# Feature stages of a two-layer decoder trunk: matmuls issued as two wide and two narrow, in place of one wide and one narrow in turn

## The reference, cut to what matters

```python
for i in range(DEPTH):                       # 2 layers
    hn = rms_norm(h, pre_mix_g[i])
    y = conformer_conv(hn, ...) if i == 0 else diff_attention(hn, ...)
    h = h + rms_norm(y, post_mix_g[i])
    u = causal_dwconv(rms_norm(h, pre_ffn_g[i]) @ ffn_w_in[i], ffn_w_dw[i])   # "up" product
    g, up = jnp.split(u, 2, axis=-1)
    f = (jax.nn.silu(g) * up) @ ffn_w_out[i]                                  # "down" product
    h = h + rms_norm(f, post_ffn_g[i])
    gate = sigmoid(rms_norm(h, ple_pre_g[i]) @ ple_w_gate[i] + ple_b_gate[i])
    h = h + rms_norm(gate * (p[i] @ ple_w_proj[i]), ple_post_g[i])
# diff_attention: q, k, v = split(x @ w_qkv); softmax(q k') twice, weighted; ... @ w_o
```

## Time and profile before

| | |
|---|---|
| time, median of three | 2470.36 us |
| time of the profiled execution | 2471.12 us |
| its span, first to last instruction | 2469.2 us |
| mean granted TensorE clock | 0.989 of full speed |
| busy: PE / PEld / DVE / ACT / POOL | 97% / 83% / 66% / 50% / 1% |
| mean busy share of the 16 DMA engines over the queue of weights | 55.6% |

### The profile page before, as it was taken

How to read it: one execution, slowest core, us unless ns; L and a number is a source line. 1 busy time by engine, 2 the same in 40 slices (tenths; PEclk the granted TensorE clock), 3 DMA queues, 4 the chain that set the end, 5 groups by cost and what they waited for, 6 DMA issues and landing times.

```text
span 2469.2 us, 38655 instructions
## 1 busy us (share of the span) xinstructions
PE 2407.0 (97%) x12274; PEld 2059.0 (83%) x12274; DVE 1632.9 (66%) x2208; ACT 1240.9 (50%) x1777; POOL 33.1 (1%) x58
## 2 busy tenths in 40 slices
PE   8999899999999999999899999999999999999997
PEld 7888678888888878878788887888888888888876
DVE  5988667777777754456655676577777777544465
ACT  3333545555555544446544455465656556444463
POOL 1000000000000000000000000000000000000000
PEclk9999999999999999999999999999999999999999
DMA  7552455566655665556475544656556656655553
GB/s 262 167 166 69 145 162 173 185 196 192 190 180 186 198 205 193 195 168 216 143 218 185 178 154 145 196 155 188 185 187 195 193 183 185 215 194 194 192 192 137
DMA packets 364721, 448.16 MB, mean 182 GB/s; under 512 B 27108, under 2 KB 273030, under 8 KB 363488
## 3 DMA queue, kind: packets, MB, share of 16 engines
q1 hardware_dynamic: 362576, 436.36, 55.6%
q0 software_dynamic: 2064, 10.79, 1.3%
HBM read 444.95 MB, written 2.10 MB: 181 GB/s over the span
## 4 chain that ended last, share of the span: by engine, by line
PE 91%; issue 4%; DVE 2%; ACT 1%; DMA 1%; POOL 0%; SPq 0%; DVEq 0%; ACTq 0%; POOLq 0%
PE ps L1343 31%; PE ps L1345 16%; PE ps L1378 11%; PE ps L1380 11%; PE ps L1379 11%; PE ps L1422 9%; PE ps L1323 1%; DMA gain<-in_post_ffn_g 1%; PE ps L1517 0%; PE ps L1531 0%; DVE h L896 0%; DVE w_lo L854 0%; PE ps L1480 0%; ACT v_conv L656 0%; ACT w_hi L542 0%
## 5 line engine op out<-in xcount | busy, mean ns | idle before, releaser
L854 DVE TENSOR_TENSOR w_lo<-raw,w_hi 128x1024 fp32r<-128x1024 f32 x760 | 925.5, 1223 | 649.4 <-ACT w_hi L542 629.6
L542 ACT CAST w_hi<-raw 128x1024 fp32r<-128x1024 f32 x760 | 792.5, 1049 | 746.6 <-PE ps L1380 378.0
L1343 PE MATMUL ps<-x,w_hi 128*128 128x512 f32 x3328 | 1161.9, 395 | 3.1 <-issue 3.1
L1345 PE MATMUL ps<-x,w_lo 128*128 128x256 f32 x3328 | 929.6, 279 | 0.0
L1343 PEld LDWEIGHTS ps<-x,w_hi 128*128 128x128 f32 x3328 | 625.4, 188 | 147.2 <-issue 4.1
L1345 PEld LDWEIGHTS ps<-x,w_lo 128*128 128x128 f32 x3328 | 629.2, 189 | 0.0
L1378 PE MATMUL ps<-w_hi,mid 128*128 128x512 f32 x704 | 274.2, 390 | 3.1 <-DVE w_lo L854 3.1
L1379 PE MATMUL ps<-w_lo,mid 128*128 128x512 f32 x704 | 274.0, 389 | 0.0
L1380 PE MATMUL ps<-w_hi,mid 128*128 128x512 f32 x704 | 274.0, 389 | 0.0
L1378 PE MATMUL ps<-w_hi,x 128*128 128x512 f32 x640 | 254.9, 398 | 7.2 <-DVE x L1051 3.8
L1379 PE MATMUL ps<-w_lo,x 128*128 128x512 f32 x640 | 250.6, 392 | 0.0
(11 more groups left out here) (160 smaller groups left out, 1278.3 us busy)
## 6 DMA issues: line engine op xcount, KB each, us to landing
raw<-in_ffn_w_in SPq DMA_DIRECT2D x704, 256.0 KB, 3.1
raw<-in_ffn_w_out SPq DMA_DIRECT2D x352, 256.0 KB, 3.5
raw<-in_attn_w_qkv SPq DMA_DIRECT2D x192, 256.0 KB, 2.9
wg<-in_conv_w_pw SPq DMA_DIRECT2D x128, 256.0 KB, 4.0
raw<-in_ple_w_gate SPq DMA_DIRECT2D x128, 256.0 KB, 3.5
raw<-in_conv_w_pw SPq DMA_DIRECT2D x64, 256.0 KB, 3.5
raw<-in_attn_w_o SPq DMA_DIRECT2D x64, 256.0 KB, 3.4
raw<-in_ple_w_proj SPq DMA_DIRECT2D x16, 256.0 KB, 3.6
```

The lines of the kernel that those rows point to most:

```text
L542: nc.scalar.copy(w_hi[:, u % RING], raw[:, u % RING]).then_inc(hi_split, 1)
L854: nc.vector.tensor_tensor(w_lo[:, u % RING], raw[:, u % RING], w_hi[:, u % RING].bitcast(F32), ALU.subtract).then_inc(split_done, 1)
L1343: mm(ps[:, 4 * s + f], w_hi[:, u % RING, q, columns], x[:, kt].rearrange("p a t -> p (a t)"), start=kt == 0, stop=False)
L1345: ins = mm(ps[:, 4 * s + f, 0:T], w_lo[:, u % RING, q, columns], x[:, kt, 0], start=False, stop=kt == KT - 1)
```

## The change

Inside a unit the eight pairs (wide, narrow) are taken two at a time. For the two pairs `a` and `b` the order wide a, narrow a, wide b, narrow b becomes wide a, wide b, narrow a, narrow b. Two neighbouring pairs always have the same input block and differ in the output block, so they write different PSUM banks. Number, shape and operands of the matmuls are unchanged, and so is the last instruction of a unit, the one that counts it as used.

```diff
-                    for q in range(UNIT_KT):
-                        kt = UNIT_KT * j + q
-                        for f in blocks:
-                            columns = slice(P * f, P * (f + 1))
-                            mm(ps[:, 4 * s + f], w_hi[:, u % RING, q, columns], x[:, kt].rearrange("p a t -> p (a t)"),
-                               start=kt == 0, stop=False)
-                            ins = mm(ps[:, 4 * s + f, 0:T], w_lo[:, u % RING, q, columns], x[:, kt, 0],
-                                     start=False, stop=kt == KT - 1)
+                    def wide(q, f):
+                        kt, columns = UNIT_KT * j + q, slice(P * f, P * (f + 1))
+                        return mm(ps[:, 4 * s + f], w_hi[:, u % RING, q, columns], x[:, kt].rearrange("p a t -> p (a t)"),
+                                  start=kt == 0, stop=False)
+
+                    def narrow(q, f):
+                        kt, columns = UNIT_KT * j + q, slice(P * f, P * (f + 1))
+                        return mm(ps[:, 4 * s + f, 0:T], w_lo[:, u % RING, q, columns], x[:, kt, 0],
+                                  start=False, stop=kt == KT - 1)
+
+                    order = [(q, f) for q in range(UNIT_KT) for f in blocks]
+                    for at_n in range(0, len(order), 2):
+                        wide(*order[at_n])
+                        wide(*order[at_n + 1])
+                        narrow(*order[at_n])
+                        ins = narrow(*order[at_n + 1])
                     return ins
```

## The result

The changed kernel takes 2477.6 us in the median of 20 runs (2474.0 to 2482.1), the kernel before 2471.7 us in the median of its 20 (2467.3 to 2475.6). The ratio is 1.0026, with a 95% interval of 1.0019 to 1.0032: slower by about 5.9 us, and clear of noise. It lies inside the forecast range and just inside the band of 0.3% that I had called the same. The forecast of exactly no change was 2470.4 us: 7.2 us too low, of which 1.3 are the median of the kernel before, which moved from 2470.4 in three runs to 2471.7 in 20.

What follows compares the result with a forecast made beforehand. The prediction took TensorE's matmul pace as the bound; 453.4 + 119.6 + 119.6 ns made 692.6 per four as before, a change of 0 and 2470.4 us against the median. Its own range was 2463 to 2478, for 8 in 10 2459 to 2490.

Steps and rivals of the forecast that it cites:

- my three outcomes: Whole kernel: the same within 0.3%, chance 0.64; slower by more, 0.22; faster by more, 0.14.
- my own test: Windows of up 0, 400 to 800 us: 2310 matmuls again; wrong if the count moves by more than 7.
- sum of zero: Four matmuls in the feature stages: 453.4 + 119.6 + 119.6 = 692.6 ns, as before, so 0 us over 1664.
- The bound: Whole kernel: TensorE sets the end for 91% of the span, the two changed lines holding 31% and 16%.
- The narrow matmul before a narrow one: New step inside a unit: its weight load stays covered, so it takes 119.6 ns as before a wide one.
- rival C: Narrow-to-narrow step: a second short slot can't cover its load; 115.5 us slower, giving 2586; chance 0.05.
- The two wide matmuls: Wide-to-wide and wide-to-narrow steps in a unit: 226.7 ns each as in the token stage, 453.4 ns for both.
- Rival A: Up stages: qk's slow rhythm of 352.5 ns a pair spreads there; 17.5 us slower, giving 2488; chance 0.18.
- Rival D: qk: loses its slow rhythm; 3.2 us faster, giving 2467; no chance of its own, counted inside the forecast's 0.62.
- Rival B: Feature stages: the fixed price belongs to changes of kind; 44.3 us faster, giving 2426; chance 0.13, whole or in part.

Runs made afterwards that it cites:

- e7: Changed kernel with VectorE's wait for the gain in the down stages moved to just ahead of its first multiplication: 2471.0 us, ratio to before 1.0002.
- e6: Kernel before with VectorE's wait for the gain in the down stages moved to just ahead of its first multiplication: 2466.1 us, ratio 0.9980.
- e3: Changed kernel with all eight wide matmuls of each unit first, then all eight narrow ones: 2477.9 us, ratio to before 1.0021.
- e9a: Kernel before with one extra 128-column transpose into an idle bank behind the first chunk of each feature stage: 2480.5 us, one run.
- e4: Changed kernel with the new order kept in qk alone and the old order in both up stages: 2471.6 us, ratio to before 1.0006.
- e13: Changed kernel with one extra transpose behind the first chunk of each feature stage: 2477.6 us, one run.

## Why the prediction was right, and where it was not

The range held the time and the likeliest of my three outcomes came, but by little, and the pace failed my own test: I had said that a count off by more than 7 in the window of up 0 would prove me wrong, and it is off by 11. The prediction was right on what bounds the kernel and on the loads; its sum of zero was wrong. That the time stayed in the range owes much to luck: a loss of 4.8 us in the up stages, a gain of 2.2 in qk and some 3 us of clock that I had not thought of.

*The bound.* Right: TensorE still holds 91% of the chain, and a pace that makes 5 us makes 5 us of time (e7 against e6, 4.8).

*The narrow matmul before a narrow one, 119.6 ns.* Right in what mattered, that its load is covered; rival C (115.5 us) is out. The step itself is 114.6 ns in the changed kernel and 120.0 in the long runs of e3. The Trainium skill's page "TensorE: Matmul & The Clock Gate", section "LDWEIGHTS (loading the stationary operand)", gives a load its columns over 1.2 GHz, an estimate of 107 ns. Two loads begun 0.11 us apart here agree with it. By the Trainium skill's section "Back-to-back issue gap" of that page, columns over 2.4 GHz plus 2.5 ns each, a pair is an estimate of 325 ns. That fits no order of the fp32r matmuls: the quickest takes 346.7.

*The two wide matmuls, 453.4 ns, and the sum.* This is the step that failed. I took the steps of like kinds from stages where like had followed like for long and added them to those of the mixed stage, as if each step had its own price. In the changed kernel the two wide steps take 232.9 + 233.3 = 466.2 ns, 12.8 more than the 453.4 of the sum, and the two narrow ones 230.4, 8.8 less than its 239.2. By the counts the four are 2 x 348.0 = 696.0 ns, not 692.6: 3.4 ns x 1408 = 4.8 us over the up stages that the sum has at nothing. Even the old pair was split wrongly, as 226.7 and 119.6 where up 0 has 230.1 and 116.6. The 226.7 of the token stage returns only from the sixth wide matmul of a run on (e3).

*Rival A.* Its mechanism is real, shown by e9a and e6: the old order has two patterns at a fixed clock. But the new order did not fall into that one; it has a pattern of its own at about a quarter of the price (1.7 for 6.2 ns), the same in ten stages of four programs (the changed kernel, e4, e7, e13). Its limit was worked out too low: 7.4 us over the 1408 fours of the up stages are 5.3 ns for four, not 4.5. *Rival D* came in at two thirds: qk gained 2.2 of the 3.2 us, by losing the slow pattern. *Rival B* is out: like after like still pays the fixed price in a long run (120.0 for 106.7 ns in e3), and what the narrow steps of the changed kernel saved, the wide ones more than took back.

*What I did not count.* The clock. I treated it as the same on both sides; it makes up to 3.3 of the 5.9 us, on runs with a scatter of 4 us either way. Nor did I see that a gain in qk can be lost again at the head of up 1, as in e4.

*Open.* What makes the patterns. They depend on the order of kinds, not of banks, and on the moment after an interruption for the old order; the series 0 or 6.2, 1.7, 4.3, 2.4 is described by a cost behind each change of kind that levels off after some five wide matmuls, but why there is such a cost is not shown. Nor is why the clock at the head of up 1 goes with the pace of qk.

## What to carry to other kernels

When an engine is the bound and the change only reorders its instructions, don't add up prices of single steps from different stages; count instructions in a long window of each stage, and look whether equal code runs at unequal pace in two stages, for then the pace may be a pattern that small things can shift. A change of under 0.5% should be judged by such counts and by runs of equal mean clock, not by medians alone; and a gain in one stage should be looked for again in the next ones, where the clock may take it back. And look for pauses too: one wait moved to its first real user took away two, of 2.2 and 0.9 us, and the kernel gained 5.1 us, about as much as the order cost; part of that came, in the profile, by way of qk's pattern.

## What the runs showed of the hardware

- In a long run of its own kind, an fp32r matmul takes its columns at 2.4 GHz plus 13.3 ns: 226.7 for 512 columns (token stage, and e3 from the sixth wide one on), 120.0 for 256 (e3 from the third narrow one on). The rows of plain float32, 216 ns each for 256 columns passed twice, don't show it.
- Behind a change of kind the steps differ from that: five wide ones behind eight narrow ones take 233, 236, 228, 233 and 231 ns, the first narrow one behind eight wide ones 113 (e3).
- A stage of alternating wide and narrow fp32r matmuls runs at 346.7 or at 353.3 ns a pair at the same granted clock of 1.00. One foreign matmul of 0.12 us behind its first chunk moved up 1 from one to the other for the next 475 us, but not up 0 or qk. The same program had the same paces in two profiles.
- The granted clock in the first 10 us of up 1 was 1.00 in the five profiles with qk at 353.3 ns a pair, and 0.75 to 0.80 in the eight with a quicker qk. The cause is open.
